# One product for two branches' scores in the second attention of a transformer kernel, with both results in one PSUM bank

## The reference

```
s_s = jnp.einsum('btgjd,bgtkd->bgtjk', qr, k_sel) * scale      # selected keys
p_s = masked_softmax(s_s, mask_s[:, :, :, None, :])
o_s = jnp.einsum('bgtjk,bgtkd->btgjd', p_s, v_sel)
s_w = jnp.einsum('btgjd,bkgd->btgjk', qr, kw_i) * scale        # window keys
p_w = masked_softmax(s_w, mask_w[None, :, None, None, :])
o_w = jnp.einsum('btgjk,bkgd->btgjd', p_w, vw_i)
o = gi[..., 0:1] * o_c + gi[..., 1:2] * o_s + gi[..., 2:3] * o_w
```

## Time and profile before

| | |
|---|---|
| median of 3 runs | 2417.26 us (2415.43 to 2419.38) |
| the profiled execution | 2417.43 us |
| its span in the profile | 2415.6 us |
| PE busy | 2378.7 us, 98% of the span |
| DVE, ACT, POOL busy | 893.8, 1048.3, 978.0 us |
| second attention's groups in the span | scores from 732.7 us, last values of the memory groups to 844.5 us |

### The profile page before, as it was taken

One profiled execution on the slowest core, in us unless ns is written; L12 is line 12 of the kernel. 1 busy time (PEld: TensorE's weight loads), 2 busy tenths in 40 slices (PEclk: granted clock), 3 DMA queues, 4 the chain that ended last, 5 costly groups with the idle time before them and its releaser, 6 DMA issues.

```text
span 2415.6 us, 36441 instructions
## 1 busy us (share of the span) xinstructions
PE 2378.7 (98%) x12861; PEld 1960.8 (81%) x12861; DVE 893.8 (37%) x1820; ACT 1048.3 (43%) x1704; POOL 978.0 (40%) x504
## 2 busy tenths in 40 slices
PE   9999999999999999999999999999999999999998
PEld 7887888888778888888888877888887797888886
DVE  7975322211577733222125244221212674211212
ACT  7575444422346744343336343432322584432421
POOL 4822444444442234444443314444443414444441
PEclk9999999999999999999999999999999999999999
DMA  4311223233310023223332212222222202222221
GB/s 157 115 35 45 95 92 100 89 111 104 124 62 11 2 70 104 97 94 104 105 106 72 86 35 79 90 102 96 96 95 79 79 10 70 96 98 97 99 98 61
DMA packets 57878, 202.95 MB, mean 84 GB/s; under 512 B 7072, under 2 KB 7968, under 8 KB 57392
## 3 DMA queue, kind: packets, MB, share of 16 engines
q1 hardware_dynamic: 54864, 196.02, 24.3%
q10 hardware_dynamic: 2912, 5.55, 0.6%
HBM read 199.44 MB, written 2.10 MB: 83 GB/s over the span
## 4 chain that ended last, share of the span: by engine, by line
PE 72%; issue 15%; POOL 7%; DVE 3%; ACT 2%; DMA 0%; POOLq 0%; DVEq 0%; ACTq 0%
PE bank L815 59%; POOL w_lo L644 7%; PE bank L1049 2%; PE bank L1032 2%; PE bank L1023 2%; PE bank L1150 1%; PE bank L1125 1%; PE bank L1136 1%; ACT h_hi L1659 1%; PE bank L1539 1%; DMA w_raw<-in_weights 0%; PE bank L1520 0%; PE bank L959 0%; POOL score L748 0%; DVE tmp L2307 0%
## 5 line engine op out<-in xcount | busy, mean ns | idle before, releaser
L644 POOL TENSOR_TENSOR w_lo<-w_raw,w_hi 128x1024 fp32r<-128x1024 f32 x368 | 885.1, 2406 | 1219.3 <-ACT w_hi L1616 1209.5
L815 PE MATMUL bank<-h_hi,w_hi 128*128 128x512 f32 x1640 | 648.1, 395 | 4.8 <-DVE tmp L2710 1.4
L815 PE MATMUL bank<-h_hi,w_lo 128*128 128x512 f32 x1640 | 639.7, 390 | 0.0
L815 PE MATMUL bank<-h_lo,w_hi 128*128 128x512 f32 x1640 | 639.5, 390 | 0.0
L1616 ACT ACTIVATE w_hi<-w_raw 128x1024 fp32r<-128x1024 f32 x368 | 386.9, 1051 | 240.3 <-PE bank L815 214.4
L815 PEld LDWEIGHTS bank<-h_hi,w_hi 128*128 128x128 f32 x1640 | 308.6, 188 | 79.1 <-issue 6.9
L815 PEld LDWEIGHTS bank<-h_lo,w_hi 128*128 128x128 f32 x1640 | 308.8, 188 | 64.9 <-issue 2.2
L815 PEld LDWEIGHTS bank<-h_hi,w_lo 128*128 128x128 f32 x1640 | 308.5, 188 | 65.0
L815 PE MATMUL bank<-mact_hi,w_hi 128*128 128x512 f32 x512 | 199.3, 389 | 1.7 <-DVEq L2573 1.7
L815 PE MATMUL bank<-mact_hi,w_lo 128*128 128x512 f32 x512 | 199.2, 389 | 0.0
L815 PE MATMUL bank<-mact_lo,w_hi 128*128 128x512 f32 x512 | 199.2, 389 | 0.0
(11 more groups left out here) (426 smaller groups left out, 3403.3 us busy)
## 6 DMA issues: line engine op xcount, KB each, us to landing
w_raw<-in_weights SPq DMA_DIRECT2D x368, 512.0 KB, 3.3
out<-x ACTq DMA_DIRECT2D x8, 256.0 KB, 2.0
x<-in_xT SPq DMA_DIRECT2D x4, 256.0 KB, 7.1
x<-in_xT ACTq DMA_DIRECT2D x4, 256.0 KB, 7.3
memx<-in_memT SPq DMA_DIRECT2D x1, 1024.0 KB, 9.9
cmp_w1k<-in_cmp_w ACTq DMA_DIRECT2D x1, 1024.0 KB, 4.9
cmp_w1v<-in_cmp_w ACTq DMA_DIRECT2D x1, 1024.0 KB, 6.5
rope_c<-in_rope_c SPq DMA_DIRECT2D x1, 256.0 KB, 8.0
```

Source lines behind the costliest of these rows:

```text
L644: nc.gpsimd.tensor_tensor(w_lo[:, t % RING, :], w_raw[:, t % RAW, :], w_hi[:, t % RING, :].bitcast(F32), ALU.subtract).then_inc(lo_ready, 1)
L815: r = nc.tensor.matmul(out, a, b, start=first and n == 0, stop=last and n == 2)
```

## The change

For query tiles 0 and 1 the two branches of a head are a pair: `first_of_pair` is the first branch's unit, `second_of_pair` the second's. The scores of both are now one product for the rounded keys and one for the rest; the moving operand takes the keys of both branches (`k[:, g:g + 3:2, 0:n]`, two runs of n columns, 1024 columns apart), and the results lie side by side in the first unit's bank. `scores_ready` rises by two at the end of the second product. The pair's first exponential waits for the maxima of both units. The pair's scores wait for the exponentials of unit n - 3 instead of n - 4, since that bank now holds two units. Tiles 2 and 3, the first attention and the memory groups are as before.

```
+def first_of_pair(unit):
+    return unit.kind == "nsa" and unit.qt < 2 and unit.branch == 1
+def second_of_pair(unit):
+    return unit.kind == "nsa" and unit.qt < 2 and unit.branch == 2
...
+        def scores_of(unit):
+            n = P * len(key_tiles(unit.kind, unit.qt))
+            if second_of_pair(unit):
+                return score_bank[(unit.n - 1) % 4][:, n:2 * n]
+            return score_bank[unit.n % 4][:, 0:n]
...
             def group_scores(unit):
+                if second_of_pair(unit):
+                    return
...
+                if first_of_pair(unit):
+                    if unit.n >= 4:
+                        pe.wait_ge(probs_ready, unit.n)
+                    both = out[:, 0:2 * n].rearrange("p (b n) -> p b n", b=2)
+                    for part, k in enumerate(k_nsa):
+                        g = unit.head // 6
+                        r = nc.tensor.matmul(both, q_nsa[:, unit.head, queries], k[:, g:g + 3:2, 0:n], start=part == 0, stop=part == 1)
+                    r.then_inc(scores_ready, 2)
+                    return
...
             def group_exponentials(unit):
-                act.wait_ge(max_ready, unit.n + 1)
+                act.wait_ge(max_ready, unit.n + 2 if first_of_pair(unit) else unit.n + 1)
...
-                nc.scalar.activation(weights, score_bank[unit.n % 4][:, 0:weights.shape[1]], ACT.Exp, bias=nmax[:, s4:s4 + 1],
+                nc.scalar.activation(weights, scores_of(unit), ACT.Exp, bias=nmax[:, s4:s4 + 1],
...
             def group_maximum(unit):
-                src = score_bank[unit.n % 4][:, 0:n]
+                src = scores_of(unit)
```

## The result

The changed kernel takes 2422.11 us (median of 13 runs, 2418.88 to 2425.32), the kernel before 2417.11 us (13 runs, 2415.37 to 2419.38). The ratio is 1.002 with a 95% interval of 1.0011 to 1.0028: it is slower, by about 5 us or 0.2%. The forecast was 2421.8 us, inside 2416.8 to 2424.4 us, and lay at the border between "within 0.2%", which it gave a chance of 0.57, and "slower", 0.40. The two medians differ by 5.0 us where the border is at 4.8, so the measurement lies at the border too, a hair on the side of "slower".

What follows compares the result with a forecast made beforehand. PE was taken to bound the kernel, so attention losses arrive one to one. 11 x (0.62 - 0.01) - 11 x 0.21 = +4.4 us on 2417.43 gave 2421.8 us, range 2416.8 to 2424.4 us.

Steps and rivals of the forecast that it cites:

- The chain of the B step: Step scoring tile 1's pair: second product, maximum, exponentials, move, values in tight sequence; PE stalls 0.62 us more each time.
- the wait for both maxima: Tile 1's step: the first exponential follows the second maximum instead of the first, 0.39 us more.
- the later scores: Tile 1's step: the first unit's scores are complete later, moving DVE's first maximum by 0.23 us.
- The A step: Step scoring tile 0's pair: four products of 128 columns become two of 256, gaining 0.20 or 0.21 us.
- The 0.14 us of slack: Tile 0's step: ACT's move is ready 0.14 us before PE's values ask for it, so the gain stays.
- rival E: Short products were cheap all along, so tile 0's step gains nothing: 2424.1 us, chance 0.06.
- rival D: Tile 0's step stalls as well; a move 0.3 us later would give 2423.6 us; chance 0.14.
- B: Tile 1's step: only the wait for both maxima counts, DVE's start isn't moved: 2419.3 us, chance 0.12.
- C: Third unit's values not held by ACT's move, stall hidden, only PE's gain left: 2415.0 us, chance 0.08.
- The first B step: Tile 1's step where the pipeline fills: counted at nothing, covered by the fill's other waits; uncovered 0.6 us.

Runs made afterwards that it cites:

- the A pair alone: The changed kernel joining only query tile 0's units (two products of 256 columns), tile 1 as before: 2414.71 us, ratio 0.9993 against the kernel before.
- the B pair alone: The changed kernel joining only query tile 1's units (two products of 512 columns): 2423.08 us, ratio 1.0029 against the kernel before.

## Why the prediction was right

*The chain of the B step.* Every stage was found where it was put: second product at 0.32, first maximum at 0.90, exponentials at 1.81, values piece 2.07 against 2.1. Expected was 0.62 us of extra stall, measured 0.60. The split into 0.39 for the wait for both maxima and 0.23 for the later scores was tested by itself: 0.35 and 0.23.

*The A step.* Gain 0.21 us as reckoned, and 0.23 a head with the A pair alone. ACT's exponentials start 1.31 us into the step and its moves 1.82, where I had 1.30 and 1.84. The 0.14 us of slack held in all A steps but one, which is treated below; so rival E fell, and D with it except for that one step.

*Rivals B and C.* B wanted the joined product to hand over no later: DVE's wait grew from 0.21 to 0.44 us. C wanted PE's stall not to hang on ACT's move: reordering ACT alone took 0.64 us a head from the changed kernel.

*What was off.* The first B step was counted at nothing, under the cover of the fill, and it cost 0.21 us. From the first 512-column product of the fill to the first A step behind it took 7.36 us (735.99 to 743.35) instead of 7.15 (734.45 to 741.60). Up to the values the cover is complete: PE's first values start 5.31 us behind that first product in both kernels (735.99 to 741.30, 734.45 to 739.76). The weights of the third unit then wait for ACT's move, as in every other B step, but for less:

```profile
741.83 1.03 PEld L1077 LDWEIGHTS bank<-v_nsa,probT_groups 128*64 128x64 f32 x32 [0.22 <-ACT probT_groups L1780]
```

With the A pair alone the stretch from that first product to the A step takes 7.15 us, with the B pair alone 7.14, and with both pairs and ACT's moves first 7.14. So it took both pairs and ACT's old order together to cost anything here, and of the 0.62 us the fill covered some 0.4.

Behind the fill the 11 heads give 11 x 0.38 = 4.2 us of the 4.4 measured between the two marks, and I had said 4.4. The other 0.2 is one A step in which DVE idled 0.23 us between its first two maxima:

```profile
777.40 0.30 DVE L2390 CUSTOM_DVE_ANT_0 bank<-bank,nsa_mask 128x128 f32<-128x128 f32 x1 [0.23 <-issue]
```

The kernel before has the same gap in the same step, at 774.10, and there it cost nothing, since ACT's moves had 0.36 us to spare. The change used that up: in this one step the weights of the values wait 0.17 us for ACT's move (778.84), and the head takes 8.48 us (771.44 to 779.92) where its neighbours take 8.20. That is what rival D described. In sum the attention grew by 4.6 us from 732.12 to 845.58 before, 733.66 to 851.71 after, against 4.4 in the prediction. That the sums agree so closely is in part luck, since the repeated steps were put 0.2 us too high and the two places left out of the sum came to 0.4 together. The profiled spans differ by 4.2 us, with 1.5 us lost ahead of the attention and 1.9 won behind it; both stretches hold the same code, and single executions of one kernel range over 4 to 6 us, so I give that no cause. The medians differ by 5.0 us.

## What to carry to other kernels

Results that share a bank were handed over together here, so the consumers started at the end of the last one, and ACT, which had begun on the first unit while DVE was at the second, now followed behind both; price that on the chain from the product to the engine's next wait, not on the producer. Joining products pays only where the short ones are no cheaper than one of double width, here two of 128 columns (0.21 us for four) and not two of 256 (7.57 us a head with that pair joined too, 7.56 without), and only if the consumers have slack; so join where both hold, not wherever the shapes allow. And on an in-order engine look at what stands behind the instruction that will wait: moving two copies ahead of two exponentials gave back more than the change had lost.

## What I had not expected of the hardware

DVE's idle time of 0.23 us, put down to "issue", stands once in the attention of each of the ten kernels profiled here, and always at the same place: between the first two maxima of the fifth A step behind the fill (774.10 before, 777.40 after). The profile names no wait of the program for it. That it keeps its place while the times shift by up to 6 us ties it to the place in the program; what causes it stays open. Whether it costs anything depends on the slack of that step alone: nothing in the kernel before, 0.28 us with the change. Products of 128 columns with a weight load each followed each other after 0.11 us, as products of 256 did after 0.12, and joining four of the first to two of the second saved 0.21 us in each A step.
